# Hybrid decoder step on one Trainium2 core: router logits and expert tokens taken from x before its norm, during the output projection, and the down bias added in the last expert group

## The chip, the cores and the metric

The kernel runs on one core of one Trainium2 chip. The metric is the device time of one execution in microseconds (us). TensorE (PE) multiplies, VectorE (DVE) and ScalarE (ACT) work elementwise and drain PSUM, GpSimd (POOL) builds constants, and SyncE (SP) issues the weight transfers, which 16 DMA engines carry out.

## The reference

One layer for 256 prompt tokens and 8 single-step samples, 264 tokens together, 1024 channels, all float32. What matters here is the stage between the mixing branches and the experts, and the experts:

```python
x = x + jnp.einsum("bld,de->ble", g_a * branch_a + g_b * branch_b, w_out)
hm = _rmsnorm(x, norm_ffn).reshape(b * l, D_MODEL)
# in _moe(hm, ...):
logits = x2d.astype(jnp.float32) @ w_router.astype(jnp.float32) + b_router.astype(jnp.float32)
top_v, top_i = lax.top_k(logits, TOP_K)
top_w = jax.nn.softmax(top_v, axis=-1)
gates = jnp.sum(jax.nn.one_hot(top_i, N_EXPERTS, dtype=jnp.float32) * top_w[..., None], axis=1)
for e in range(N_EXPERTS):
    gu = x2d @ w_gate_up[e] + b_gate_up[e]
    gate = jnp.minimum(gu[:, :D_FF], SWIGLU_LIMIT)
    up = jnp.clip(gu[:, D_FF:], -SWIGLU_LIMIT, SWIGLU_LIMIT)
    hid = (up + 1.0) * (gate * jax.nn.sigmoid(SWIGLU_ALPHA * gate))
    ye = hid @ w_down[e] + b_down[e]
    out = out + gates[:, e:e + 1] * ye.astype(jnp.float32)
```

`_rmsnorm` divides a token by the root of the mean of its squares and multiplies by a gain per channel. 4 of 32 experts are taken per token. After the experts come a gated per-layer embedding and a last norm.

## The kernel before

**Layout.** Activations stand transposed: 128 channels on the partitions, 8 blocks `k` of channels, 264 tokens along the free side (`xT`, `aT`, `zT`). For the router and the gather they are also wanted with tokens on the partitions: three blocks `j` of 88 tokens (`TB`, `NTB`).

**PSUM.** Each of the 8 banks has a written-out order of uses (`plan(name, bank)`); `to_fill` waits until the bank's use before is drained, `fill_done` tells that it is filled, and `to_drain` and `wait_drained` are the other side. On DVE and ACT nearly every instruction is followed by a wait for itself (`tell`, `out_of`).

**Weights.** A ring of 12 slots of 1 MB. SP issues the loads in order. Three slots serve `w_in`, `w_conf_out`, `w_gdn_out` and `w_out`; the other nine are filled with the first chunks of experts 0 and 1 from load 32 of the stream on, and the last three follow as chunks of `w_out` come free (L539 to L541). From then on each load waits for the chunk that held its slot 12 loads ago (`chunk_used`). An expert is 12 chunks: 8 of `w_gate_up`, 4 of `w_down`. The loads of group 1 and later first wait for `order_ready` (L543), since the order of the experts is data.

**Between the branches and the experts.** PE computes `wo`, the output projection, as eight blocks of eight matmuls (L846), one bank each. DVE adds each block to `xT` (L1642), ACT squares it (L1111). Then, each after the one before: PE sums the squares over channels by a matmul with ones (L612), ACT takes the root (L1117), DVE the reciprocal and the eight normed blocks `aT` (L1392, L1394). PE computes the logits as 24 matmuls with 88 x 128 weights (L863) and transposes `aT` into 88-token blocks (L870), which ACT copies to `hm_tok` (L1286). DVE adds the router bias and takes the top four (L1650 to L1662, `sel`), ACT exponentiates (L1290), DVE normalizes to `gates`. PE transposes the gates (L875), counts each token's rank within its expert (L883, L885), and multiplies the 32 x 264 gates with the down biases `b_down`, eight matmuls that DVE adds to `xT` (L891, L1755). DVE builds one-hot rows of the ranks (L1693), and PE gathers the 64 tokens of each of the first two experts (L907). ACT makes a rounded copy of the gate-up bias (L1292), DVE the low part (L1759). DVE then picks the two busiest experts and their places (L1769 to L1790), which gives `order_ready`.

**Experts.** 17 groups: 15 of two experts with 64 token slots each, and groups 6 and 11 with one expert and 128 slots. In a group PE adds the bias (L929), multiplies with the gate-up chunks (L937: x as weights of 64 columns, one expert on either half of the array), gathers for the next group (L907), transposes the hidden rows (L948), adds the outputs of the group before back to their tokens (L990, the scatter, in two parts), and multiplies with the down chunks (L969). DVE clips and multiplies, and adds the scattered rows to `xT` (L1749).

## Time and profile before

| | us |
|---|---|
| median of 3 runs | 1619.56 (1614.94 to 1626.01) |
| the profiled execution | 1626.19 |
| its span, first to last instruction | 1624.5 |
| PE busy | 1480.3 (91%) |
| DVE busy | 505.9 (31%) |
| ACT busy | 251.7 (15%) |
| POOL busy | 49.0 (3%) |
| HBM read | 455.75 MB |

Times of instructions are from the start of the span. Overlapping matmuls are each given their whole pass through the array, so a group's busy time, or the distance between starts, tells more of its price than the mean of one. A float32 matmul shows as two instructions, a float32 transpose as one.

### The profile page before, as it was taken

What the parts mean: (1) busy time and instruction counts of PE and PEld (TensorE: products, weight loads), DVE (VectorE), ACT (ScalarE), POOL (GpSimd) and SP (SyncE); (2) the same over time, 40 slices, a digit from 0 to 9 for tenths busy, and PEclk for the clock granted to TensorE, in tenths of its full rate; (3) what the DMA queues carried; (4) which work ended last, traced back from release to release, by engine and by line L of the source; (5) the groups of instructions that cost most, each with busy time, mean ns of one, the idle gap of its engine ahead of it and who ended that gap; (6) DMA issues with size and microseconds to landing.
All of it is one profiled execution on the core that took longest, in us unless ns stands there. A gap on an engine that the chain in (4) does not pass through costs nothing.

```text
span 1624.5 us, 19637 instructions
## 1 busy us (share of the span) xinstructions
PE 1480.3 (91%) x7317; PEld 863.8 (53%) x7317; DVE 505.9 (31%) x1074; ACT 251.7 (15%) x502; POOL 49.0 (3%) x68
## 2 busy tenths in 40 slices
PE   3899999889999799989989999998999999889777
PEld 3587777677788644433443444444344434424356
DVE  1366677786521321211210221121022102202222
ACT  2341424223220201000100100010010101001022
POOL 2010101111000000000000000000000000000000
PEclk8798999999999779999999999999999999999989
DMA  6132414232259149999999999999998999999920
GB/s 181 52 105 66 121 53 133 68 105 90 79 185 333 49 201 420 421 422 423 421 422 422 421 381 357 421 422 422 422 421 352 386 421 421 422 423 421 407 71 27
DMA packets 120447, 462.62 MB, mean 285 GB/s; under 512 B 9783, under 2 KB 68680, under 8 KB 71128
## 3 DMA queue, kind: packets, MB, share of 16 engines
q1 hardware_dynamic: 100304, 447.97, 68.9%
q10 hardware_dynamic: 20080, 13.82, 3.0%
q8 instruction: 39, 0.64, 0.2%
q14 instruction: 24, 0.20, 0.0%
HBM read 455.75 MB, written 6.68 MB: 285 GB/s over the span
## 4 chain that ended last, share of the span: by engine, by line
PE 71%; DMA 14%; DVE 9%; ACT 2%; issue 2%; ACTq 1%; SPq 0%; POOL 0%; DVEq 0%; POOLq 0%
PE bank L937 19%; PE bank L969 15%; DMA ring<-in_w_gate_up 14%; PE bank L802 9%; PE bank L907 6%; PE bank L846 4%; PE bank L990 4%; PE bank L674 2%; PE bank L1034 2%; DVE lent L1570 1%; PE bank L612 1%; PE bank L929 1%; ACTq L1065 1%; PE bank L680 1%; PE bank L948 1%
## 5 line engine op out<-in xcount | busy, mean ns | idle before, releaser
L937 PE MATMUL bank<-ring,lent 128*64 128x512 f32 x2176 | 482.3, 596 | 50.2 <-DMA ring<-in_w_gate_up 50.1
L937 PEld LDWEIGHTS bank<-ring,lent 128*64 128x64 f32 x2176 | 159.0, 137 | 365.1 <-issue 348.1
L969 PE MATMUL bank<-ring,lent 128*64 128x512 f32 x1088 | 241.0, 595 | 0.2 <-ACT lent L1324 0.2
L802 PE MATMUL bank<-lent,ring 128*128 128x264 f32 x896 | 237.7, 410 | 3.4 <-DVE big L1591 1.6
L802 PEld LDWEIGHTS bank<-lent,ring 128*128 128x128 f32 x896 | 172.2, 203 | 38.8 <-issue 8.0
L1731 DVE TENSOR_SCALAR big<-bank 128x512 f32<-128x512 f32 x34 | 21.9, 686 | 476.9 <-PE bank L937 476.9
L969 PEld LDWEIGHTS bank<-ring,lent 128*64 128x64 f32 x1088 | 75.1, 137 | 143.5 <-issue 135.9
L1318 ACT ACTIVATE big<-big 128x512 f32<-128x512 f32 x34 | 20.9, 630 | 545.1 <-DVE big L1731 545.1
L907 PEld LDWEIGHTS bank<-st,big 88*128 88x128 f32 x816 | 97.3, 200 | 14.5 <-issue 14.5
L907 PE MATMUL bank<-st,big 88*128 88x128 f32 x816 | 100.6, 286 | 0.8 <-DVE xT L1755 0.8
L1749 DVE TENSOR_TENSOR xT<-xT,bank 128x264 f32<-128x264 f32 x136 | 58.3, 429 | 102.5 <-PE bank L990 100.9
L990 PE MATMUL bank<-outputs 128*128 128x264 f32 x272 | 69.5, 401 | 1.2 <-ACT outputs L1310 1.2
L674 PEld LDWEIGHTS bank<-ring 128*128 128x128 f32 x448 | 61.9, 205 | 14.5 <-DVE ring L1482 9.0
L1686 DVE CAST selector<-eye_order 64x64 fp32r (+1 forms) x32 | 4.9, 186 | 206.7 <-PE bank L937 206.7
L674 PE MATMUL bank<-ring 128*128 128x128 f32 x448 | 63.7, 290 | 5.9 <-DVE ring L1482 4.8
L1570 DVE SCALAR_TENSOR_TENSOR lent<-lent,wdw 128x256 f32<-128x256 f32 x120 | 63.2, 527 | 4.3
L1310 ACT COPY outputs<-bank 128x512 f32<-128x512 f32 x34 | 18.2, 588 | 295.1 <-PE bank L969 295.1
L990 PEld LDWEIGHTS bank<-outputs 128*128 128x128 f32 x272 | 50.5, 195 | 22.4 <-issue 13.0
L846 PE MATMUL bank<-lent,ring 128*128 128x264 f32 x192 | 43.2, 387 | 1.1 <-DVE lent L1639 1.1
L846 PEld LDWEIGHTS bank<-lent,ring 128*128 128x128 f32 x192 | 36.3, 190 | 7.7 <-DVE lent L1639 1.5
L1034 PE MATMUL bank<-lent,ring 128*128 128x264 f32 x128 | 32.3, 409 | 4.4 <-DVE lent L1394 4.4
L680 PE MATMUL bank<-ident,ring 128*128 128x128 f32 x128 | 20.6, 290 | 13.6 <-DVE ring L1476 9.3
(304 smaller groups left out, 1104.6 us busy)
## 6 DMA issues: line engine op xcount, KB each, us to landing
ring<-in_w_gate_up SPq DMA_DIRECT2D x256, 1024.0 KB, 17.5
ring<-in_w_down SPq DMA_DIRECT2D x128, 1024.0 KB, 23.4
ring<-in_w_in SPq DMA_DIRECT2D x28, 1024.0 KB, 5.3
st<-in_state_gdn ACTq DMA_DIRECT2D x8, 512.0 KB, 5.6
out<-st ACTq DMA_DIRECT2D x8, 512.0 KB, 3.5
ring<-in_w_gdn_out SPq DMA_DIRECT2D x4, 1024.0 KB, 5.2
ring<-in_w_out SPq DMA_DIRECT2D x4, 1024.0 KB, 10.8
ring<-in_w_ple_gate SPq DMA_DIRECT2D x4, 1024.0 KB, 17.6
```

Of the source, the lines that this page charges most:

```text
L674: last = mm(b[:, i * P:(i + 1) * P], lhs(i), rhs(i), start=True, stop=True)
L680: last = tr(b[:, i * P:(i + 1) * P], src(i), ident[:])
L802: last = mm(b[:, 0:T], w[:, k, o:o + P], aT[:, k, :], start=k == 0, stop=k == KD - 1)
L846: last = mm(b[:, 0:T], w[:, k, o:o + P], rhs(k), start=k == 0, stop=k == n_k - 1)
L907: last = mm(aux[h][:, i * SLOTS:(i + 1) * SLOTS], hm_tok[0:TB, j, k * P:(k + 1) * P], onehot[:, j, :], start=j == 0, stop=j == NTB - 1)
L937: last = mm(bank[t][rows, :], x_slots[:, c, rows], w, start=False, stop=c == KD - 1)
L969: last = mm(bank[4 + t][rows, :], hT[:, m, rows], w, start=m == 0, stop=m == KD - 1)
L990: mm(bank[SCATTER_BANKS[i]][:, 0:T], y[:, i * P:(i + 1) * P], spread, start=True, stop=True).then_inc(sm["sc_filled"], 1)
L1034: last = mm(b[:, 0:T], w[:, k, P * (i % 2):P * (i % 2) + P], aT[:, k, :], start=k == 0, stop=k == KD - 1)
L1570: tell(v.scalar_tensor_tensor(x, up[:, i, tap:tap + TP], w, x, ALU.mult, ALU.add), "conf_done" if t == CK * CB - 1 else None)
L1731: v.tensor_scalar(half(gbuf, h), bank[h][:], LIMIT, None, ALU.min).then_inc(sm["gate_in"], 1)
L1749: v.tensor_tensor(xT[:, i, :], xT[:, i, :], bank[SCATTER_BANKS[i]][:, 0:T], ALU.add).then_inc(sm["sc_added"], 1)
```

## The change

- `wo` uses banks 0 and 1 in turn. After each block PE transposes the block before it. What is transposed is `xg`, which ACT makes of `xT` and the gain `norm_ffn`, without the root (`tokens_of`, 3 transposes a block).
- The logits are made of `xg` with `w_router` as weights of 32 columns; block `k` goes to columns and PSUM rows 32 (k mod 4). DVE copies the four partial rows to `lq`, and three short matmuls with a stacked identity (`eye4`) add and transpose them.
- DVE squares and sums over the blocks during `wo`; the sum over channels is six matmuls that move two columns. ACT takes the root of 88 x 3 values and DVE the reciprocal. The factor enters as the scale of the six `hm_tok` copies and of the logits.
- The rounded bias and its low part are made while `wo` runs; DVE waits for it at block 3.
- The ranks come before the gates, with seven matmuls in place of nine; the offset `FAR` stays in the ranks and in `iota`, which takes away a DVE instruction. The gates are finished, and transposed, behind the first gather in PE's order.
- The matmuls of the down bias move into the last group, one behind each pair of gate-up chunks, and DVE adds them there. `b_down` lies elsewhere and is loaded after the exponentials.

```diff
-        for name in ("bb", "ba", "wo"):
+        for name in ("bb", "ba"):
             for i in range(KD):
                 plan(f"{name}{i}", i)
+        for i in range(KD):
+            plan(f"wo{i}", i % 2)
...
-            dense("wo", "out", 2, KD, lambda k: aT[:, k, :])
-            sum_squares("rms2", 2)
+            def tokens_of(k):
+                pe.wait_ge(s["xg_ready"], k + 1)
+                for j in range(NTB):
+                    name = f"hm{2 * j + k // 4}"
+                    b = to_fill(pe, name) if k % 4 == 0 else bank[uses[name][0]][:]
+                    x = tr(b[0:TB, (k % 4) * P:(k % 4 + 1) * P], xg[:, k, j * TB:(j + 1) * TB], ident[:])
+                    if k % 4 == 3:
+                        fill_done(name, x)
+            def raw_logits(b, k):
+                q = slice(NE * (k % 4), NE * (k % 4 + 1))
+                return mm(b[q, 0:T], wr[:, k, :], xg[:, k, :], start=k < 4, stop=k >= 4)
+            for i in range(KD):
+                w = take_chunk(pe, "out", i // 2)
+                b = to_fill(pe, f"wo{i}")
+                o = P * (i % 2)
+                for k in range(KD):
+                    last = mm(b[:, 0:T], w[:, k, o:o + P], aT[:, k, :], start=k == 0, stop=k == KD - 1)
+                fill_done(f"wo{i}", last)
+                if i:
+                    tokens_of(i - 1)
+            lqb = to_fill(pe, "lq")
+            for k in range(KD - 1):
+                raw_logits(lqb, k)
+            pe.wait_ge(s["xg_ready"], KD)
+            fill_done("lq", raw_logits(lqb, KD - 1))
+            pe.wait_ge(s["squares"], KD + 1)
+            b = to_fill(pe, "ss")
+            for j in range(NTB):
+                cols_j = slice(j * TB, (j + 1) * TB)
+                mm(b[0:TB, 2 * j:2 * j + 2], sq_sum[:, cols_j], ones[:, 0:2], start=True, stop=False)
+                last = mm(b[0:TB, 2 * j:2 * j + 2], sq_last[:, cols_j], ones[:, 0:2], start=False, stop=True)
+            fill_done("ss", last)
+            tokens_of(KD - 1)
+            wait_drained(pe, "lq")
             b = to_fill(pe, "logits")
             for j in range(NTB):
-                for k in range(KD):
-                    if j == 0:
-                        wait_block(2, k)
-                    last = mm(b[0:TB, j * NE:(j + 1) * NE], aT[:, k, j * TB:(j + 1) * TB], wr[:, k, :],
-                              start=k == 0, stop=k == KD - 1)
+                last = mm(b[0:TB, j * NE:(j + 1) * NE], lq[:, j * TB:(j + 1) * TB], eye4[:], start=True, stop=True)
...
+            pe.wait_ge(s["selected"], 1)
             b = to_fill(pe, "rank")
...
-            for i in range(KD):
-                b = to_fill(pe, f"bd{i}")
-                fill_done(f"bd{i}", mm(b[:, 0:T], b_down[:, i * P:(i + 1) * P], gatesT[:], start=True, stop=True))
...
+            def down_bias(i):
+                if i >= 2:
+                    pe.wait_ge(s["bd_added"], i - 1)
+                mm(aux[i % 2][:, 0:T], b_down[:, i * P:(i + 1) * P], gatesT[:],
+                   start=True, stop=True).then_inc(s["bd_filled"], 1)
...
+                    if end:
+                        if c == 0:
+                            pe.wait_ge(s["bd_loaded"], 16 * 3)
+                        down_bias(c)
...
             gather(first, 0)
+            pe.wait_ge(s["gates"], 1)
+            b = to_fill(pe, "gTr")
+            for j in range(NTB):
+                last = tr(b[0:NE, j * TB:(j + 1) * TB], gates[:, j, :], ident[0:TB, 0:TB])
+            fill_done("gTr", last)
             pe.wait_ge(s["bias_ready"], 1)
...
             act.wait_ge(s["mix"], KD)
-            act.dma_start(b_down, a["b_down"][0]).then_inc(s["bd_loaded"], 16)
...
-            squares(zT, lambda k: wait_drained(act, f"wo{k}"))
-            root(rstd[:], "rms2", 1.0 / D)
+            for k in range(KD):
+                wait_drained(act, f"wo{k}")
+                A(xg[:, k, :], xT[:, k, :], ACT.Copy, scale=par[:, 8 + k:9 + k]).then_inc(s["xg_ready"], 1)
+                if k == 1:
+                    act.wait_ge(s["bd_loaded"], 16 * 2)
+                    nc.scalar.copy(bias, b_stage).then_inc(s["b_high"], 1)
+                if k == 2:
+                    tell(A(small8[:, 3:4], small8[:, 0:1], ACT.Sqrt, scale=0.0))
+            out_of(A(root_t, to_drain(act, "ss")[0:TB, 0:2 * NTB].rearrange("t (j two) -> t j two", two=2)[:, :, 0],
+                     ACT.Sqrt, bias=eps[0:TB, 0:1], scale=1.0 / D), "ss")
+            act.wait_ge(s["rstd_ready"], 1)
...
+                if end:
+                    dve.wait_ge(sm["sc_added"], n * KD - KD)
+                    for i in range(KD):
+                        dve.wait_ge(s["bd_filled"], i + 1)
+                        v.tensor_tensor(xT[:, i, :], xT[:, i, :], bank[6 + i % 2][:, 0:T], ALU.add).then_inc(s["bd_added"], 1)
+                    dve.wait_ge(s["bd_added"], KD)
                 dve.wait_ge(sm["chunk_used"], at * RING + (2 * KD if kind == PAIR else KD))
```

## Rows read from the trace of the kernel before

**Rows 1.** The page: 40 slices of 40.6 us, DMA busy in tenths, and GB/s
```profile
DMA  6132414232259149999999999999998999999920
GB/s 181 52 105 66 121 53 133 68 105 90 79 185 333 49 201 420 421 422 423 421 422 422 421 381 357 421 422 422 422 421 352 386 421 421 422 423 421 407 71 27
```
**Rows 2.** The chain that ended last, in the experts: start us, us, what
```profile
698.96 22.41 DMA ring<-in_w_gate_up
...
758.58 22.46 DMA ring<-in_w_gate_up
...
1315.39 27.62 PE bank L937 x128
```
**Rows 3.** Timeline, 480 to 600 us: start, us, engine, line, op, shapes, count, idle before
```profile
504.93 28.75 PE L846 MATMUL bank<-lent,ring 128*128 128x264 f32 x128 [1.06 <-DVE lent L1639]
...
530.22 0.43 DVE L1642 TENSOR_TENSOR xT<-xT,bank 128x264 f32<-128x264 f32 x1 [3.13 <-PE bank L846]
...
533.51 3.72 PE L612 MATMUL bank<-big,ones 128*128 128x264 f32 x16
...
541.67 7.93 PE L863 MATMUL bank<-wr,lent 128*88 128x32 f32 x48 [4.43 <-DVE lent L1394]
...
549.42 4.14 PE L870 MATMUL bank<-ident,lent 128*88 128x128 f32 x24
549.74 0.63 DVE L1650 TENSOR_TENSOR st<-bank,brt 88x32 f32<-88x32 f32 x3 [5.39 <-PE bank L863]
...
552.41 0.25 DVE L1662 TENSOR_TENSOR st<-st 88x96 f32<-88x96 f32 x1
...
557.07 1.90 ACT L1292 CAST moe<-big 64x2048 fp32r<-64x2048 f32 x1
...
558.23 0.62 PE L875 MATMUL bank<-ident,st 88*32 88x88 f32 x3 [4.67 <-DVE st L1667]
...
561.73 7.40 PE L891 MATMUL bank<-outputs,big 32*128 32x264 f32 x16
...
562.66 0.62 DVE L1693 TENSOR_TENSOR st<-st 88x192 f32<-88x192 f32 x2
...
569.70 2.28 DVE L1759 TENSOR_TENSOR moe<-big,moe 32x2048 fp32r<-32x2048 f32 x1
...
569.92 10.36 PE L907 MATMUL bank<-st,big 88*128 88x128 f32 x47 [0.79 <-DVE xT L1755]
...
581.22 2.04 PE L929 MATMUL bank<-moe,selector 64*128 64x512 f32 x4 [0.72 <-issue]
...
588.40 4.24 SPq L504 DMA_DIRECT2D ring<-in_w_gate_up  x4
```
**Rows 4.** Issues of DMA at 505 us: KB each, median us to landing
```profile
big<-in_b_gate_up ACTq DMA_DIRECT2D x2, 256.0 KB, 8.7
```
**Rows 5.** Stretches of 1 us: busy of PE, PEld, DVE, ACT, POOL, granted clock, DMA, GB/s
```profile
541.00:542.00 1.00, 0.33 (x3) 0.25 (x3) 0.97 (x3) 0.00 (x0) 0.00 (x0) 0.97 0.00 0
...
552.00:553.00 1.00, 1.00 (x10) 0.98 (x9) 0.59 (x4) 0.70 (x3) 0.00 (x0) 0.91 0.00 0
...
555.00:556.00 1.00, 0.00 (x0) 0.00 (x0) 0.00 (x0) 1.00 (x1) 0.00 (x0) 0.80 0.00 0
...
586.00:587.00 1.00, 1.00 (x8) 0.26 (x6) 0.00 (x0) 0.00 (x0) 0.00 (x0) 0.84 0.00 0
```
**Rows 6.** Timeline, group 15, at the full clock
```profile
1462.03 5.62 PE L907 MATMUL bank<-st,big 88*128 88x128 f32 x48
...
1475.79 0.39 PE L984 MATMUL bank<-ident,st 88*128 88x88 f32 x3
```
**Rows 7.** Chain, 250 to 260 us: a product of 128 columns that moves 512
```profile
257.61 1.91 PE bank L791 x4
```
**Rows 8.** Timeline, last group
```profile
1521.88 1.29 DVE L1731 TENSOR_SCALAR big<-bank 128x512 f32<-128x512 f32 x2 [44.58 <-PE bank L937]
...
1537.62 10.52 PE L969 MATMUL bank<-ring,lent 128*64 128x512 f32 x48
```

More of the change, by code:

```diff
@@ L52 @@
 BIG = 3.0e38
+FAR = 10000.0
 CHUNK_COLS = 2048
@@ L884, in _ @@
+            mm(b[0:TB, NE:3 * NE], before[:], sel[:, 1:3, :].rearrange("t j e -> t (j e)"), start=True, stop=False)
+            mm(b[0:TB, NE:3 * NE], ones[0:TB, 0:TB], sel[:, 0, :].unsqueeze(1).broadcast_to([TB, 2, NE]), start=False, stop=False)
+            mm(b[0:TB, 2 * NE:3 * NE], ones[0:TB, 0:TB], sel[:, 1, :], start=False, stop=True)
             for i in range(NTB):
@@ L917, in wait_loaded, with group @@
                 pe.wait_ge(sems[slot], at * 16 + 16 * (i // RING + 1 + prefilled[slot]))
-            def group(sm, sems, prefilled, n, at, kind, first, last_one):
+            def down_bias(i):
[3 more added lines that the diff above has]
+                   start=True, stop=True).then_inc(s["bd_filled"], 1)
+            def group(sm, sems, prefilled, n, at, kind, first, last_one, end=False):
                 experts = 2 if kind == PAIR else 1
@@ L1007, in _ @@
             n = GROUPS - 1
-            group(first, loaded, slot_fills, n, round_of(n, shift_of(n)), PAIR, False, True)
+            group(first, loaded, slot_fills, n, round_of(n, shift_of(n)), PAIR, False, True, True)
             last_scatter(first, GROUPS)
@@ L1709, in pair_halves, with group @@
                 return [(pos, low), (pos + 1, low)]
-            def group(sm, n, at, kind, halves, after, first, last_one):
+            def group(sm, n, at, kind, halves, after, first, last_one, end=False):
                 own = [0]
@@ L1752, in _ @@
             make_selector(first, eye2, 0, 1)
-            for i in range(KD):
-                b = to_drain(dve, f"bd{i}")
-                out_of(v.tensor_tensor(xT[:, i, :], xT[:, i, :], b[:, 0:T], ALU.add), f"bd{i}")
-            dve.wait_ge(s["b_high"], 1)
-            low_rows = slice(NE, 2 * NE)
-            tell(v.tensor_tensor(bias[low_rows], b_stage[low_rows], bias[low_rows].bitcast(FP32), ALU.subtract), "bias_ready")
+            b = to_drain(dve, "rank")
+            out_of(v.tensor_copy(count_row, b[0:TB, NTB * NE:(NTB + 1) * NE]), "rank")
+            dve.wait_ge(s["wexp"], NTB)
+            tell(v.tensor_tensor(gates[:], gates[:], sel[:], ALU.mult))
+            tell(v.tensor_reduce(wsum[:], gates[:], AX.X, ALU.add))
+            tell(v.reciprocal(wsum[:], wsum[:]))
+            tell(v.tensor_tensor(gates[:], gates[:], wsum[:].unsqueeze(2).broadcast_to([TB, NTB, NE]), ALU.mult), "gates")
             wait_drained(dve, "gTr")
@@ L1770, in _ @@
                 for other in WIDE_AT[:i]:
-                    tell(v.memset(key[:, other:other + 1], -far))
+                    tell(v.memset(key[:, other:other + 1], -FAR))
                 tell(v.tensor_reduce(key_max[:], key[:, FREE:], AX.X, ALU.max))
```

115 lines of the change are left out of this document (58 added, 57 removed).

## The prediction

> **What bounds the kernel.** I read the page by slices first, then the chain that ended last, then the timeline of the one place where both DMA and PE stand low. From 609 us to about 1540 us the DMA engines move 421 to 423 GB/s, with a dip at each of the two wide groups [rows 1]. The chain says the same from the other side: a pair group ends in a wait for a gate-up chunk, and these waits lie 758.58 - 698.96 = 59.62 us apart, which is 24 chunks of 1 MB at 2.48 us, 422 GB/s [rows 2]. PE at full clock would need less: 27.62 us for the gate-up part of a group, about 53 us with the rest [rows 2]. So the expert phase is a fixed amount of transfer behind one starting point. Where PE leads it (around the wide groups), PE too started from that point.
>
> The starting point is the first load behind the prefilled ring, issued at 588.40 us, when PE has used the first pair of chunks [rows 3]. Slices 14 and 15 show what lies before it: 49 and 201 GB/s [rows 1]. The projection ends at 504.93 + 28.75 = 533.68 us. From there to 588.40 are 54.7 us in which nearly nothing is loaded, and whatever comes off them comes off the end. That the stream is the bound afterwards makes this certain, since no engine has to be faster later.
>
> **The change, part by part.** I keep the old times and call T the end of the projection, 533.7.
>
> *In the projection.* Six groups of three transposes now stand inside it. At full clock three of nearly this form took 0.39 [rows 6], so 6 x 0.39 = 2.3; at low clock 24 took 4.14 [rows 3], so 3.1. Each needs the block before added (0.43) and scaled (about the same, an ACT pass over 264 columns), against a block of 28.75 / 8 = 3.6 [rows 3]: ready. Two banks in place of eight also suffice for the same reason. DVE gets three passes a block, 1.3 of some 4.0. At block 3 it waits for ACT's rounded bias: loads issued at 505.3 land 8.7 later [rows 4], at 514, ACT's 1.9 ends near 517, block 3 is there at 520. DVE's low part of 2.3 [rows 3] then fits before block 4 plus one. If it didn't, two banks would stall PE by at most those 2.3. Root table and one-time loads hide here too. New end of the projection: T' = 536.0.
>
> *Behind it on PE.* Three transposes, 0.4. Then eight raw logits, 16 instructions moving 264 columns. One after another they cost what the projection's do, 28.75 / 128 = 0.225 each, 3.6. On column tiles they may overlap: 512 columns cost 1.91 / 4 = 0.48 in the form with 128 columns [rows 7] and 27.62 / 128 = 0.22 on two halves [rows 2], a factor of two shown. Four tiles give 0.9 at best. I take 1.5, nearer to the overlapped end, because that row has the same mechanism. The last block is scaled at T' + 1.1, before its turn. At T' + 1.9 follow the sums of squares, 12 instructions with 88-column weights: L863's took 7.93 / 48 = 0.165, some of it waits [rows 3], so 1.3 to 2.0, taken as 1.5. With the last three transposes T' + 3.8. Beside them run the copy of the partial logits (0.43), the root (0.3) and the reciprocal (0.2). The three short products, six instructions of the same kind, 1.0, bring it to T' + 4.9 with a signal of 0.1.
>
> *The choice.* DVE needed 549.74 to 552.66 [rows 3], 2.9; two small instructions move out of the way, 2.6 left: T' + 7.5. The ranks no longer wait for the gates. Before, 21 instructions for gates and ranks ran from 558.23 to 561.73 [rows 3], 0.17 each; 14 now, two of them twice as wide, 2.6: T' + 10.2. Rank and one-hot on DVE, 0.25 + 0.62 + 0.1 [rows 3]: T' + 11.2 = 547.2. The `hm_tok` copies, six of 0.6 from T' + 4.2, are done by T' + 8. The exponentials (table 1.3, then 1.0) and gates end beside the gather, so they cost nothing; without that cover they would cost the 4.7 of idle PE that stood before L875 [rows 3].
>
> *Gone from here:* the sum of squares (3.7), root, reciprocal and first normed block (4.4 idle), the logits (7.9), the transposes (4.1), 4.7 of wait for gates, and the down bias (7.4) [rows 3]. The gather starts at 547.2 in place of 569.92: **22.7 earlier**.
>
> *Added behind the gather.* ACT's order is gates first, gathered tokens second. The first half of the tokens was copied during the gather; now both wait behind the transposes of the gates: 0.62 [rows 3], gates copy 0.37, and one more copy of 0.58. So **1.5 later**. DVE selects the wide experts after the gates' copy, near 559 to 567; its order is needed only for chunk 24, twelve chunks behind the first load, near 590, so it stays hidden. Leaves 21.2 for the first load.
>
> *Last group.* PE waits for gate-up chunks there, so seven of the eight products (0.45 each, 264 columns twice) lie in waits. The last stands behind the last chunk, and DVE adds before it clips: 0.45 + 0.1 + 0.43. DVE started its clip at 1521.88, released by PE's last gate-up product [rows 8], and from here PE and not DMA runs the chain: 10.52 us of down products follow [rows 8] with their chunks landed. So **1.0 later**.
>
> Sum: 22.7 - 1.5 - 1.0 = 20.2. The profiled execution took 1626.19, so 1606.0; it stood 6.6 above the median of the runs, and against that median, 1619.56, I forecast **1599.4**.
>
> **The clock.** The granted clock fell at 541.9 us, 4.7 us after PE had ended its sum of squares at 537.2, rose at 552.2, fell at 555.6 in the wait for the gates, and rose only at 586.3, three us into the first gate-up products [rows 5] (each worked out from the mean of the microsecond in which it changed). The whole gather ran at 1.2 GHz: 10.36 us against 5.62 at 2.4 GHz [rows 3, 6]. The sum keeps it so, since the new order too has a DVE wait of 2.6 and one of 1.0 just before it. If the clock held, the gather would give 4.7, bias 0.8, first chunks 1.5, and small ones 0.3: 7.3 more.
>
> **The rivals.**
>
> *A, the forecast*, 1594 to 1604: chance 0.62.
>
> *B, the clock holds through the gather*: 20.2 + 7.3 = 27.5, time 1592. For it: the waits are shorter than the 4.4 and 4.7 before. Against it: even 20 us of nearly unbroken PE work, 561.7 to 581, did not bring the clock back. 0.12.
>
> *C, the tiles don't overlap and the projection stretches*: raw logits 3.6 in place of 1.5, DVE's bias work 2.3, transposes 0.8: 5.2 less, time 1604.6. For it: no row shows 32-column tiles. 0.13.
>
> The Trainium skill (TensorEngine Tiling (Array Packing), Tiling Modes, Key Properties) says that changing the tiling mode drains the engine, and that tiles within a mode run in parallel. It speaks against putting one short tiled piece between full-width ones; with its best case the raw logits cost 0.9 and with no overlap 3.6, the two ends used above from rows.
>
> *D, part of the gain is not carried through*, by the last group (a clip later by several us because DVE's adds queue up) or by a transfer: time 1606 to 1616. Against it: DMA is busy in all slices after the start. 0.09.
>
> *E, the other side: the clock stays low far into group 0.* PE then needs 2 x 53 = 106 us a pair group, DMA 59.62, so each us at low clock starves the stream of 0.44. From 20.2 / 0.44 = 46 us of it on the kernel is slower; one low group costs 47, time 1646. Against it: the clock rose three us into the same instructions [rows 5]. 0.04.
>
> The Trainium skill (TensorE: Matmul & The Clock Gate, Seeing it yourself) reports a clock seen stuck low for over 50 us; no row here shows that.
>
> **How the numbers follow.** The likeliest case gives 1599.4. At best, B with the tiles at 0.9 and the sums at 1.3, 28.3 come off, 1591; at worst, C with the sums at 2.0, 14.5, 1605. The three runs before spread 11 us around their median, so I add half of that above and a little below: 1588 to 1611. One per cent, 16.2 us, is what a measurement can tell: faster by more means under 1603.4: all of B, nearly all of A, two fifths of C, 0.12 + 0.60 + 0.05 = 0.77; D and the rest of A and C within, 0.18; E and a tail of D slower, 0.05.
>
> **What would show it.** In the changed profile: projection 31 us in place of 28.75; under 13 us from its end to the gather; raw logits near 1.5; gather 10.4 (A) or 5.6 (B); the first load behind the ring near 567; 59.6 between pair groups unchanged; clip in the last group 1 us behind the last chunk. The forecast is wrong if a wait stands at block 3 of the projection, if the first load is not earlier by as much as the end is, or if the clock's low stretch changes its length.

## The result: 1599.03 us, and the profile after

| | before | after |
|---|---|---|
| median of 4 runs, us | 1618.16 (1614.94 to 1626.01) | 1599.03 (1596.92 to 1602.02) |
| the profiled execution, us | 1626.19 | 1598.15 |
| its span | 1624.5 | 1596.3 |
| ratio of the runs | | 0.9876, 95% interval 0.9836 to 0.9916 |

The changed kernel is faster by 1.2% (0.8 to 1.6%); small, but the interval excludes no gain. Of the two profiled executions one span is 28.2 us shorter than the other, more than the 19.1 us between the medians; the sections below take that apart.

The page of the changed kernel, 40 slices of 39.9 us, answers to [rows 1]:

```profile
DMA  6132324232249289999999989999998999999920
GB/s 184 49 110 67 111 66 123 67 106 83 67 159 370 87 349 421 421 422 422 422 422 422 421 348 390 421 421 422 422 422 346 389 422 422 422 422 421 412 93 28
```

The stream is the same, 421 and 422 GB/s with two dips. Slice 15, 201 GB/s before, has become 349. The stage in front of it, timeline of the changed kernel (start us, us, engine, line, operation, shapes, count), answers to [rows 3]:

```profile
503.52 7.39 PE L882 MATMUL bank<-lent,ring 128*128 128x264 f32 x32 [1.06 <-DVE lent L1689]
...
520.19 2.28 DVE L1707 TENSOR_TENSOR moe<-big,moe 32x2048 fp32r<-32x2048 f32 x1
...
522.68 0.43 DVE L1696 TENSOR_TENSOR xT<-xT,bank 128x264 f32<-128x264 f32 x1 [0.21 <-PE bank L882]
...
530.52 3.73 PE L882 MATMUL bank<-lent,ring 128*128 128x264 f32 x16
...
534.50 1.52 PE L875 MATMUL bank<-outputs,wr 128*32 128x264 f32 x16
...
536.91 0.51 PE L868 MATMUL bank<-ident,outputs 128*88 128x128 f32 x3
...
537.26 0.58 PE L902 MATMUL bank<-eye,outputs 128*88 128x32 f32 x6
...
540.47 0.25 DVE L1726 TENSOR_TENSOR st<-st 88x96 f32<-88x96 f32 x1
...
541.91 1.47 PE L913 MATMUL bank<-st,ones 88*128 88x32 f32 x6
...
544.55 10.58 PE L930 MATMUL bank<-st,big 88*128 88x128 f32 x48 [1.17 <-DVE st L1749]
...
557.33 2.04 PE L959 MATMUL bank<-moe,selector 64*128 64x512 f32 x4 [1.76 <-ACT lent L1354]
...
564.00 4.25 SPq L511 DMA_DIRECT2D ring<-in_w_gate_up  x4
```

The projection (L882) runs from 503.52 to 530.52 + 3.73 = 534.25. DVE's low part of the bias (L1707) ends at 522.47, just before block 4 is there at 522.68, and PE does not wait. Raw logits (L875), last transposes (L868), joined logits (L902), choice (L1726) and ranks (L913) follow, and the gather (L930) starts 10.3 us behind the projection; before it was 36.2. The gather takes 10.58 us, as long as before, where all its 48 instructions take 10.58 too (the row in [rows 3] holds 47 of them and 10.36). The first load behind the ring is issued at 564.00.

The granted clock, in stretches of 1 us of the changed kernel, answers to [rows 5]:

```profile
540.00:541.00 1.00, 0.18 (x2) 0.21 (x3) 0.82 (x5) 0.97 (x2) 0.00 (x0) 0.96 0.00 0
...
561.00:562.00 1.00, 1.00 (x6) 0.38 (x4) 0.93 (x3) 0.00 (x0) 0.00 (x0) 0.80 0.00 0
```

It fell to 1.2 GHz at 540.9 and came back at 561.4: one low stretch of 20.5 us in place of two, 541.9 to 552.2 and 555.6 to 586.3, 41.0 us together.

The tail of the changed kernel, the chain from the last gate-up products on (start us, us, what), answers to [rows 8]:

```profile
1493.75 3.65 PE bank L967 x16
1497.41 0.65 PE bank L946 x2
...
1498.08 0.44 DVE xT L1789
...
1498.55 1.29 DVE big L1793 x2
...
1504.99 3.67 PE bank L1024 x12
...
1532.20 3.81 PE bank L619 x16
...
1540.44 5.49 PE bank L1075 x16
```

The same chain in the kernel before:

```profile
1518.18 3.67 PE bank L937 x16
...
1521.88 1.29 DVE big L1731 x2
...
1528.33 4.45 PE bank L990 x12
...
1556.68 6.70 PE bank L612 x16
...
1567.81 6.25 PE bank L1034 x16
```

The down bias (L946) and its add (L1789) are on the chain: the clip (L1793) comes 4.80 us behind the start of the last gate-up products, before 3.70. But three PE steps behind it are shorter, the scatter (3.67 for 4.45), the sum of squares (3.81 for 6.70) and the first gate block (5.49 for 6.25), none of which the change touches.

### The profile page after: what moved, and what is told of

It reads as the page before. It is cut to its first block, busy times and chain, and to the rows that moved or that the text cites. A ratio compares the mean times of both kernels' runs of the same rounds, so it can differ in the third digit from the quotient of the medians.

```text
span 1596.3 us, 19577 instructions
## 1 busy us (share of the span) xinstructions
PE 1462.8 (92%) x7283; PEld 847.4 (53%) x7283; DVE 507.9 (32%) x1080; ACT 253.2 (16%) x503; POOL 49.7 (3%) x71
## 4 chain that ended last, share of the span: by engine, by line
PE 72%; DMA 14%; DVE 8%; ACT 2%; issue 2%; ACTq 1%; SPq 0%; POOL 0%; DVEq 0%; POOLq 0%
PE bank L967 19%; PE bank L1003 15%; DMA ring<-in_w_gate_up 14%; PE bank L809 9%; PE bank L930 6%; PE bank L1024 4%; PE bank L853 3%; PE bank L681 2%; PE bank L1075 2%; PE bank L882 2%; DVE lent L1620 1%; PE bank L959 1%; ACTq L1106 1%; PE bank L687 1%; PE bank L982 1%
## 5 line engine op out<-in xcount | busy, mean ns | idle before, releaser
L809 PE MATMUL bank<-lent,ring 128*128 128x264 f32 x896 | 237.2, 410 | 3.3 <-DVE big L1641 1.6
L809 PEld LDWEIGHTS bank<-lent,ring 128*128 128x128 f32 x896 | 171.8, 202 | 38.4 <-issue 8.1
L1793 DVE TENSOR_SCALAR big<-bank 128x512 f32<-128x512 f32 x34 | 21.9, 686 | 430.6 <-PE bank L967 430.5
L930 PEld LDWEIGHTS bank<-st,big 88*128 88x128 f32 x816 | 97.3, 200 | 14.3 <-issue 14.3
L930 PE MATMUL bank<-st,big 88*128 88x128 f32 x816 | 100.6, 286 | 1.2 <-DVE st L1749 1.2
L1075 PE MATMUL bank<-lent,ring 128*128 128x264 f32 x128 | 31.5, 402 | 4.4 <-DVE lent L1444 4.4
L687 PE MATMUL bank<-ident,ring 128*128 128x128 f32 x128 | 20.2, 287 | 13.0 <-DVE ring L1526 9.3
L1224 ACT COPY ring<-bank 128x512 f32<-128x512 f32 x20 | 11.7, 586 | 126.1 <-PE bank L687 126.1
L882 PE MATMUL bank<-lent,ring 128*128 128x264 f32 x128 | 29.7, 387 | 1.1 <-DVE lent L1689 1.1
```

The source lines that it names most:

```text
L687: last = tr(b[:, i * P:(i + 1) * P], src(i), ident[:])
L809: last = mm(b[:, 0:T], w[:, k, o:o + P], aT[:, k, :], start=k == 0, stop=k == KD - 1)
L882: last = mm(b[:, 0:T], w[:, k, o:o + P], aT[:, k, :], start=k == 0, stop=k == KD - 1)
L930: last = mm(aux[h][:, i * SLOTS:(i + 1) * SLOTS], hm_tok[0:TB, j, k * P:(k + 1) * P], onehot[:, j, :], start=j == 0, stop=j == NTB - 1)
L1075: last = mm(b[:, 0:T], w[:, k, P * (i % 2):P * (i % 2) + P], aT[:, k, :], start=k == 0, stop=k == KD - 1)
```

## The experiments

The ledger below is read from every profile in the same way: start of the output projection, start of the first gather, first load behind the ring, start of the last gate-up products, end of the span. Each row is one execution, in us.

| kernel | projection starts at | to gather | to first load | first load to last gate-up | from there to the end | span |
|---|---|---|---|---|---|---|
| before | 504.93 | 64.99 | 83.47 | 929.78 | 106.32 | 1624.5 |
| e1, before again | 503.83 | 65.00 | 83.49 | 930.01 | 106.07 | 1623.4 |
| after | 503.52 | 41.03 | 60.48 | 929.75 | 102.55 | 1596.3 |
| e2, one column tile | 503.54 | 43.50 | 63.38 | 930.17 | 102.91 | 1600.0 |
| e3, bias ahead of group 0 | 499.31 | 41.10 | 68.79 | 929.79 | 103.81 | 1601.7 |
| e4, wide fillers | 498.88 | 39.90 | 52.26 | 932.02 | 107.84 | 1591.0 |
| e5, gates first | 504.16 | 46.13 | 65.87 | 929.99 | 107.18 | 1607.2 |
| e6, two orders mended | 499.58 | 41.11 | 59.70 | 930.03 | 105.89 | 1595.2 |
| e7, e4 and e6 and tail | 503.43 | 39.91 | 51.84 | 930.68 | 101.65 | 1587.6 |
| e8, before with fillers | 495.31 | 61.74 | 80.24 | 929.82 | 109.53 | 1614.9 |
| e9, narrow fillers | 503.94 | 40.48 | 61.11 | 929.90 | 105.45 | 1600.4 |
| e10, before, bias last | 503.10 | 58.74 | 77.47 | 930.39 | 102.94 | 1613.9 |

The second and third columns count from the projection's start. The fourth hardly moves: 929.75 to 930.7 in eleven of twelve, 932.0 in one. The first and the fifth move by up to 9.6 and 7.9 us, also between kernels whose code there is the same. The second and third repeat within 0.02 us in the two profiles of the kernel before.

**e1: the kernel before, profiled again.** No edit.

> The kernel before, profiled a second time, unchanged. In the first pair of profiles the changed kernel gained 23.0 us between the start of the output projection and the first load behind the ring, nothing from there to the last gate-up chunk (929.78 and 929.75 us), and 3.8 us in the tail behind that chunk, where I had forecast a loss of 1.0. Theory 1 (the tail's gain is the phase of PE's clock in that one execution): this second profile has a tail, from the last gate-up product to the end of the span, that differs from the first one's 106.3 us by more than a microsecond, and shows the sum of squares behind the experts at 3.8 in place of 6.7 us or the like. Theory 2 (the change causes the gain): the tail is 106.3 within 0.5 again. Under both the stretch from projection start to first load is 83.5 within 1, and the stream 929.8 within 1.

Measured: the stage 83.49 and the stream 930.01, as both theories had it. The tail is 106.07, 0.25 from the first profile, and its sum of squares 6.73. So theory 1's test failed: two executions of one kernel agreed. Theory 2 could claim it until e5, whose tail code is that of the changed kernel and whose chain reads

```profile
1539.15 6.84 PE bank L619 x16
...
1550.42 6.32 PE bank L1075 x16
```

with a tail of 107.18, against 3.81 and 5.49 in the changed kernel and the same 3.81 and 5.49 in e2, whose tail code is the same again. The short tail is no property of the change. Added up from stretches of 1 us, the clock stood low for some 27 us of the tail in e5 and in the kernel before, and for 17 to 18 in the changed kernel and in e2.

**e2: the raw logits on one column tile.**

```diff
-                q = slice(NE * (k % 4), NE * (k % 4 + 1))
-                return mm(b[q, 0:T], wr[:, k, :], xg[:, k, :], start=k < 4, stop=k >= 4)
+                return mm(b[0:NE, 0:T], wr[:, k, :], xg[:, k, :], start=k == 0, stop=k == KD - 1)
```

(the copy to `lq` and the joining products take 32 rows)

> The changed kernel with all eight raw logit products on column tile 0, accumulated in 32 rows of PSUM, in place of four tiles. Theory 1 (tiles overlap): the group took 1.52 us on four tiles and takes 3.6 us on one (16 instructions at the projection's 0.225), so the sums of squares, the logits, the gather and the first load all come 2.1 us later. Theory 2 (the last block's arrival sets it, or the moving side runs at the same rate anyway): it stays within 0.5 us of 1.52 and nothing moves.

Timeline of e2:

```profile
534.52 3.75 PE L874 MATMUL bank<-outputs,wr 128*32 128x264 f32 x16
```

3.75 for 1.52 us, the gather 2.47 later, the first load 2.9, the span 3.7 longer than that of the changed kernel (its tail is 0.4 longer). The tiles overlap. Of the 1.52 us in the changed kernel, 0.3 are a wait for ACT's scaling of the last block (L1325 ends at 535.34, the last product's weights follow); on one tile that block is there in time. The gather moves by slightly more than the products' 2.23.

**e3: the down bias back ahead of group 0**, behind the first gather:

```diff
             pe.wait_ge(s["bias_ready"], 1)
+            pe.wait_ge(s["bd_loaded"], 16 * 3)
+            wait_drained(pe, "gTr")
+            for i in range(KD):
+                if i >= 4:
+                    pe.wait_ge(s["bd_added"], i - 3)
+                mm(bank[2 + i % 4][:, 0:T], b_down[:, i * P:(i + 1) * P], gatesT[:],
+                   start=True, stop=True).then_inc(s["bd_filled"], 1)
+            pe.wait_ge(s["bd_added"], KD)
```

(DVE adds them there; they are gone from the last group)

> The changed kernel with the down bias taken out of the last group and put behind the first gather, ahead of group 0 (eight products into banks 2 to 5, added by DVE). Theory 1 (what stands before the first load costs the end one for one, and the bias in the last group costs 1.1): the eight products take 7.4 us at the low clock, some 1.7 of which hide the copies of the gathered tokens, so the first load comes 5.7 us later, the clip in the last group 1.1 earlier, and the execution is 4.6 us longer. Theory 2 (the products in the last group keep the clock up and so gain in the tail): the tail behind the last gate-up product goes from 102.5 back to 106.3 in addition, some 8.4 us longer in all.

```profile
551.99 7.37 PE L1043 MATMUL bank<-outputs 32*128 32x264 f32 x16 [0.55 <-ACT outputs L1347]
...
559.88 2.07 PE L959 MATMUL bank<-moe,selector 64*128 64x512 f32 x4 [0.52 <-DVE xT L1825]
```

The products take 7.37 us (timeline of e3). The first load comes 8.3 later, 2.6 more than expected: group 0 starts 6.8 later, since less of the products was hidden than the 1.7 I had set, and from there to the load it took 8.22 in place of 6.67, because the clock was still low at 567. The clip is 3.70 behind the last gate-up products again, 1.1 earlier. The tail is 103.8, not 106.3 or more. The median of four is 1604.92, ratio to before 0.9905 (0.9868 to 0.9942). Theory 1 holds, with its size too small; theory 2 falls.

**e4: wide fillers in PE's waits.**

```diff
+            b = to_fill(pe, "rank")
+            for i in range(6):
+                mm(b[:, 0:T], ident[:], aT[:, i, :], start=True, stop=True)
             pe.wait_ge(s["selected"], 1)
...
             fill_done("rank", last)
+            b = to_fill(pe, "gTr")
+            for i in range(2):
+                mm(b[:, 0:T], ident[:], aT[:, i, :], start=True, stop=True)
...
             fill_done("gTr", last)
+            for i in range(3):
+                mm(bank[3][:, 0:T], ident[:], aT[:, i, :], start=True, stop=True)
```

(`b` is the bank that the next real product overwrites)

> The changed kernel with products whose results are thrown away in PE's three waits: six between logits and ranks, two between ranks and gather, three behind the transposes of the gates (128 x 128 identity by 264 tokens, 0.45 us each at full clock). Theory 1 (the idle time at 537.8 to 540.8 is what drops the clock at about 540.9): the clock stays up, the ranks take 1.8 in place of 2.6, the gather 5.6 in place of 10.6, the bias products 1.2 in place of 2.0 and the first pair of chunks 3.7 in place of 4.7; the first load comes 7 us earlier and the end with it. Theory 2 (small products such as ranks and gather drop the clock whatever stands between them): the gather is still 10.4 to 10.6 and, as fillers at the low clock are twice as long, the first load is 0 to 2 us later.

Timeline of e4:

```profile
536.77 0.83 PE L915 MATMUL bank<-st,ones 88*128 88x32 f32 x6
...
538.78 5.60 PE L935 MATMUL bank<-st,big 88*128 88x128 f32 x48 [0.20 <-DVE st L1756]
...
546.37 1.17 PE L964 MATMUL bank<-moe,selector 64*128 64x512 f32 x4 [0.39 <-ACT lent L1361]
```

A stretch of 1 us just before the gather (columns as in [rows 5]):

```profile
538.00:539.00 1.00, 0.80 (x5) 0.42 (x4) 0.95 (x5) 0.96 (x3) 0.00 (x0) 1.00 0.00 0
```

The clock stays up, although PE still stands for a fifth of this microsecond. The gather takes 5.60 and the first load comes 8.2 us earlier. This is the price of the low clock in the changed kernel, up to the first load. At the last gate-up products 5.95 of the 8.22 are left (932.02 for 929.75 in the stream). Of four executions the median is 1593.44, ratio 0.9818 (0.9774 to 0.9861); the profiled one lost 5.3 of its gain in the tail, where its sum of squares took 6.86.

**e5: the gates ahead of the ranks.**

```diff
             fill_done("logits", last)
+            pe.wait_ge(s["gates"], 1)
+            b = to_fill(pe, "gTr")
+            for j in range(NTB):
+                last = tr(b[0:NE, j * TB:(j + 1) * TB], gates[:, j, :], ident[0:TB, 0:TB])
+            fill_done("gTr", last)
...
             gather(first, 0)
-            pe.wait_ge(s["gates"], 1)
...
```

(DVE finishes the gates before it takes the ranks)

> The changed kernel with the gates finished and transposed ahead of the ranks, as before, in place of behind the first gather. Theory 1 (hiding the exponentials beside the ranks and the gather is a term of its own): PE waits until the gates at 545.3 in that trace, then transposes of the gates 0.6, ranks 2.6, one-hot 1.0: the gather starts 5.2 us later; behind it the gates' transposes and copy are gone, 1.0 to 1.5 earlier; the first load comes 3.7 to 4.2 later. Theory 2 (ACT's copies of the tokens set the gather's start anyway, so the order of gates costs nothing): the first load moves by less than 1.

```profile
546.13 0.62 PE L908 MATMUL bank<-ident,st 88*32 88x88 f32 x3 [7.66 <-DVE st L1732]
```

PE stands for 7.66 us (timeline of e5) and the gather starts 5.1 later. Behind it 1.3 come back up to group 0, and 1.6 go again because the first gate-up products run longer at the low clock: the first load is 5.4 later. Theory 1 holds; the expectation left the clock out.

**e6: the two losses mended.** ACT copies the gathered tokens before the gates, and `down_bias(c)` stands ahead of the wait for chunk pair `c`:

```diff
-            out_of(nc.scalar.copy(gatesT, to_drain(act, "gTr")[0:NE, 0:T]), "gTr")
             gathered(first, 0)
+            out_of(nc.scalar.copy(gatesT, to_drain(act, "gTr")[0:NE, 0:T]), "gTr")
...
                 for c in range(KD):
+                    if end:
+                        if c == 0:
+                            pe.wait_ge(s["bd_loaded"], 16 * 3)
+                        down_bias(c)
                     for x in range(experts):
```

> The changed kernel with the two terms that my sum had as losses put right: ACT copies the gathered tokens before the gates, and in the last group each product of the down bias stands ahead of its chunk's wait in place of behind its products. Theory 1 (both losses are order alone): from the gather's start to the first load 18.3 in place of 19.45 us, and from the last gate-up product's start to the clip 3.7 in place of 4.8. Theory 2 (the extra products and PE's transposes of the gates cost what they cost wherever they stand): both stay.

From the gather to the first load 18.59 (59.70 - 41.11) in place of 19.45, and the clip 3.77 behind the start of the last gate-up products in place of 4.80. Theory 1 holds, in one execution: both losses were a matter of order, to within 0.3 and 0.1 us of its figures.

**e7: e4 and e6, and nine fillers in each of three waits of the tail.**

```diff
+                elif end:
+                    pe.wait_ge(s["bd_added"], KD)
+                    fill_time(aux[0], 9)
...
             sum_squares("rms3", 2)
+            fill_time(to_fill(pe, "pg0"), 9)
...
             sum_squares("rms4", 3)
+            fill_time(to_fill(pe, "y00"), 9)
```

(`fill_time(b, n)`: n products of the 128 x 128 identity by 264 columns of a constant into bank `b`)

> e6 and e4 together, and thrown-away products in three waits of the tail (nine each: behind the last gate-up product, between the sum of squares and the gates of the embedding, and before the last transposes). Theory 1 (in the tail as ahead of the experts the waits of 3 to 5 us drop the clock, at a point that differs from execution to execution): first load 8.2 + 1.1 earlier than in the changed kernel, counted from the projection's start; last scatter 2.7, sum of squares 3.8 and first gate block 3.6 us in every execution, tail 98.5 to 99.5 in place of 102.5; the median near 1585. Theory 2 (the fillers delay as much as the clock gives in the tail): tail 102 or more, median 1590 or more.

The chain of e7:

```profile
1495.79 2.67 PE bank L1038 x12
...
1522.45 6.71 PE bank L625 x16
...
1533.59 3.80 PE bank L1092 x16
```

The scatter (2.67) and the first gate block (3.80) run at 2.4 GHz behind their fillers. The sum of squares, whose own wait of 3.6 us I had left open, takes 6.71, with the clock low from 1521.5 to 1528.3, so the tail is 101.65 and not 99.5. The fillers stand in three waits, and the clock was up behind each set; behind the third the last transposes end 4.8 us after they start, in the changed kernel 6.3. It fell in the wait of 3.6 us that has none. Theory 1 comes out for two of its three figures and for the median, and not for the sum of squares and the tail; theory 2 asked for a median of 1590 or more. The median of six is 1585.98 (1584.07 to 1589.38), ratio to before 0.9778 (0.9756 to 0.98). Against the same measure of the changed kernel, 0.9876 in other runs, that is another 1% off. It is the lowest ratio of the kernels here, but its interval touches that of e4 (0.9774 to 0.9861), so that the two orders of e6 and the fillers of the tail gain anything beside e4 is not shown by the totals.

**e8: the kernel before with wide fillers alone**, nine ahead of its logits and twelve ahead of the gates' transposes.

> The kernel before, with thrown-away products alone: nine behind its sum of squares and twelve ahead of the gates' transposes. This asks how much of the old 54.7 us was the clock and how much the order of work. Theory 1 (the old stage was slow largely by the clock): logits, transposes, ranks and down bias and gather run at 2.4 GHz, 2.9 + 1.5 + 1.1 + 3.5 + 4.8 us and 2.3 for the first products of group 0, some 16 us earlier first load, median near 1606. Theory 2 (weight loads and DVE set these steps, so the clock matters for the gather and group 0 alone): 7 us, median near 1615.

Timeline of e8:

```profile
531.96 7.06 PE L870 MATMUL bank<-wr,lent 128*88 128x32 f32 x48 [0.34 <-DVE lent L1402]
538.84 4.70 PE L877 MATMUL bank<-ident,lent 128*88 128x128 f32 x24
...
550.61 5.63 PE L899 MATMUL bank<-outputs,big 32*128 32x264 f32 x16
...
557.05 10.58 PE L915 MATMUL bank<-st,big 88*128 88x128 f32 x48 [0.82 <-DVE xT L1763]
```

Four stretches of 1 us of e8 (columns as in [rows 5]):

```profile
534.00:535.00 1.00, 0.88 (x7) 0.65 (x7) 0.74 (x2) 0.00 (x0) 0.00 (x0) 1.00 0.06 16
535.00:536.00 1.00, 1.00 (x15) 1.00 (x15) 0.00 (x0) 0.00 (x0) 0.00 (x0) 0.96 0.00 0
...
542.00:543.00 1.00, 1.00 (x8) 0.94 (x7) 0.09 (x1) 0.73 (x2) 0.00 (x0) 0.62 0.00 0
...
553.00:554.00 1.00, 1.00 (x4) 0.77 (x3) 0.93 (x3) 0.00 (x0) 0.00 (x0) 0.50 0.00 0
```

Only 3.2 us off the stage, ratio 0.9989 (0.997 to 1.0007), no measurable gain in the total. The long wait before L870 is gone (0.34 us is left of 4.43), and within the logits PE stood only for 0.1 to 0.2 us in each of the three microseconds in which DVE was still making the normed blocks. Yet the clock fell at 535.9, four us into the logits, with PE busy throughout that microsecond; it rose at 542.8, within the transposes of `aT`, and fell again at 553, in the middle of the down bias. Neither theory foresaw this: the long wait for DVE is not needed for a fall.

**e9: narrow fillers**, the test of that sentence. As e4, with

```diff
+            for i in range(17):
+                mm(b[0:TB, 0:NE], ident[:, 0:TB], ones[:, 0:NE], start=True, stop=True)
```

and 6 and 9 of them in the two later places.

> e4 with small products in place of wide ones in the same three waits, for about the same busy time: 17, 6 and 9 products of 88 columns that move 32 (the shape of the logits in the kernel before) in place of 6, 2 and 3 of 128 columns that move 264. Theory 1 (PE's idle time drops the clock): it stays up, the gather takes 5.6 us and the first load comes 52 us after the projection's start, as in e4. Theory 2 (a stretch filled only with products of this shape drops the clock as idle time does; in e8 it fell four us into the logits although PE had not stood still before them): the clock falls at about the same place as in the changed kernel, the gather takes 10.6 us, and the first load is at 60 to 62 us.

Timeline of e9:

```profile
538.11 2.83 PE L908 MATMUL bank<-ones,ident 128*88 128x32 f32 x34
...
544.42 10.59 PE L935 MATMUL bank<-st,big 88*128 88x128 f32 x48
```

Two stretches of 1 us of e9 (columns as in [rows 5]):

```profile
541.00:542.00 1.00, 0.79 (x10) 0.79 (x10) 0.32 (x2) 0.97 (x2) 0.00 (x0) 1.00 0.00 0
542.00:543.00 1.00, 1.00 (x10) 1.00 (x9) 0.03 (x1) 0.98 (x2) 0.00 (x0) 0.69 0.00 0
```

The clock fell at 542.4 (0.69 = 0.38 x 1 + 0.62 x 0.5) in a microsecond in which PE was busy throughout, 1.5 us later than in the changed kernel. Counted from the end of the projection it fell 7.7 us on, in the changed kernel, e2, e3, e5 and e6, which have no fillers, 6.3 to 6.9, and in e4 and e7, with the wide ones, not at all. The gather took 10.59 us, as without any filler, and the first load came 61.11 behind the projection's start: e4 52.26, the changed kernel 60.48. In this trace PE being busy was not enough: it was busy in every microsecond from 543 to 562, all of them at 1.2 GHz. With the wide products of e4 the clock stayed up, with the narrow ones it fell. Theory 2 holds, theory 1 falls, in one execution of e9. The two sets of fillers differ in their data too (activations in e4, ones in e9); the wide fillers of e7's tail move a constant, and the clock was up behind all three sets, which speaks for the shape, but shape and data were not separated in these three waits.

**e10: the kernel before with the down bias in the last group**, one part of the change alone.

```diff
-            pe.wait_ge(s["bd_loaded"], 16 * 3)
-            wait_drained(pe, "gTr")
-            for i in range(KD):
-                b = to_fill(pe, f"bd{i}")
-                fill_done(f"bd{i}", mm(b[:, 0:T], b_down[:, i * P:(i + 1) * P], gatesT[:], start=True, stop=True))
...
+                    if end:
+                        if c == 0:
+                            pe.wait_ge(s["bd_loaded"], 16 * 3)
+                        down_bias(c)
```

(`down_bias` and DVE's adds as in the changed kernel)

> One part of the change alone: the kernel before with the down bias in the last group. Theory 1 (this part is worth its own time ahead of the gather and nothing else): the gather starts 6.6 us earlier (64.99 us after the projection's start becomes 58.4: 7.4 of products and 0.8 of the last drain, less what DVE's one-hot needed behind the ranks), the first load too (83.5 becomes 76.9), and the clip in the last group is 1.1 later. Theory 2 (DVE's low part of the gate-up bias, 2.3 us, which ran beside the gather, moves onto the path, or the gather now runs at the full clock since nothing cold stands before it): 74.5 or less with a gather of 5.6, or 79 or more.

Timeline of e10:

```profile
558.74 1.47 PE L883 MATMUL bank<-st,ones 88*128 88x32 f32 x6
...
561.84 10.58 PE L900 MATMUL bank<-st,big 88*128 88x128 f32 x48 [1.63 <-DVE st L1697]
562.05 2.28 DVE L1765 TENSOR_TENSOR moe<-big,moe 32x2048 fp32r<-32x2048 f32 x1
```

The gather starts 58.74 behind the projection's start, 6.3 earlier than before; the first load 77.47, 6.0 earlier. Theory 1 holds for both, within 0.6 us: DVE's low part of the bias (L1765) still runs beside the gather, as in the kernel before, and the gather still takes 10.58. The clip stands 4.80 behind the last gate-up products, 1.1 later. One execution took 1615.67, beside 1616.56 for the kernel before, so the total alone says nothing of a gain; the ledger does. Of the 23.0 us that the first load moved, 6.0 are the down bias, measured alone; the other 17.0 are the rest of the change, of which e2 and e5 take back two parts (2.9 and 5.4 us).

## Why the forecast came out

By its own steps, each in the two profiled executions and counted from the start of the projection:

| step | forecast, us | measured, us |
|---|---|---|
| projection longer | 2.3 | 2.0 (28.75 to 30.73) |
| raw logits | 1.5 | 1.52 |
| sums of squares | 1.5 | 1.1 |
| joining products | 1.0 | 0.58 |
| DVE's choice | 2.6 | 2.77 |
| ranks | 2.6 | 2.56 |
| rank and one-hot | 1.0 | 1.06 |
| end of projection to gather | 11.2 | 10.3 |
| gather earlier | 22.7 | 23.96 (64.99 - 41.03) |
| lost behind the gather | 1.5 | 0.97 (19.45 - 18.48) |
| first load earlier | 21.2 | 22.99 (83.47 - 60.48) |
| lost in the last group | 1.0 | 1.10 (4.80 - 3.70) |
| sum | 20.2 | 21.9 |

**The starting point.** This step carried the forecast, and it held: from the first load to the last gate-up products it is 929.78 us before and 929.75 after. Whatever moved the load moved the last gate-up products within 1 us, in every kernel of the ledger but e4, where 2.3 of 8.2 us were given back on the way (932.02); where, was not followed.

**The projection.** The worry at block 3 was unfounded by a narrow margin: L1707 ended at 522.47, and DVE took block 4 at 522.68, as soon as PE had it. DVE had 0.2 us to spare there, and PE no wait.

**The tiles.** The guess of 1.5 lay between 0.9 and 3.6, and e2 measured what one tile costs, 3.75. So four tiles ran 2.5 times as fast (3.75 / 1.52). Rival C asked for no overlap; e2 is that part of it, and it stood 2.9 us later at the first load, where 2.1 had been worked out. The Trainium skill (TensorEngine Tiling (Array Packing), Overview, Theoretical Speedup) gives up to 4x for a dimension of at most 32; the 2.5 measured here lies below it. Of the 1.52 us, 0.3 are the wait for the last scaled block, so without it, by subtraction, the products would take 1.2, a factor of 3.1. The drain that it names for a change of mode (same page, Tiling Modes, Key Properties) did not show as a gap of any size: the raw logits started 0.25 us after the projection's end, with three transposes between.

**The end of the projection to the gather** came out 0.9 shorter than forecast. Two terms were too large, the sums of squares (1.1 for 1.5) and the joining products (0.58 for 1.0), and both by one price: 12 and 6 short instructions at L863's 7.93 / 48 = 0.165 us [rows 3]. I had put a part of that down to waits, which is right: until 544.4 DVE was still making the normed blocks, and PE began 6 or 7 instructions a microsecond; e8, at full clock, shows the same 6 or 7 until DVE is done. The other part I had left out: L863 ran at 1.2 GHz nearly from its start, since the clock fell at 541.9. Behind DVE's last block it did 9 a microsecond, and the same line in e8 did 15 at full clock (535 to 536). The new products wait for nothing of this kind and run ahead of the fall: 1.1 / 12 = 0.09 and 0.58 / 6 = 0.10. The rank products, priced by rows at the low clock and run at it, came out as forecast; in e4, at the high one, the last six of them took 0.83 in place of 1.47.

**Behind the gather** I took 1.5 for the gates in front of the copy; e6, which turns the two around, gives 0.86 (19.45 - 18.59) for the same order. The net loss of 0.97 is close to that.

**The last group**, 1.0 forecast and 1.10 measured, is confirmed from three sides: e3 (without it) 3.70, e6 (products put ahead of the wait) 3.77, e10 (with it, in the kernel before) 4.80.

**The clock.** Case A kept the gather at 1.2 GHz, and it took 10.58 us. Case B, the clock held, did not come by itself; e4 brought it about, and its price was 8.2 us, where 7.3 had been worked out. But the reason I gave was half of it. I had the waits for DVE down as the cause. e4 filled them with wide products and the clock stayed up; e9 filled them with narrow ones, and e8 filled the long wait in the kernel before, and in both it fell while PE was busy. So neither the waits alone nor PE's busy time tells when it falls, and what PE runs in them matters. The columns moved do not sort the cases either: in e8 the clock fell a second time within the down bias, products of 32 rows that move 264 columns, and in e8 and in the kernel before it rose within the transposes of `aT`, 88 columns of weights that move 128 (at 542.8 and 552.2). What it is about the products that matters, the runs do not show. The 20 us of nearly unbroken work before the change, 561.7 to 581, that did not bring the clock back are of the same kind as the 19 in e9 (543 to 562). D and E did not come: no part of the gain was lost to the stream, and the clock rose at 561.4, four us into group 0.

**The signs I had named.** No wait stood at block 3 of the projection. The two other signs that were to show the forecast wrong did appear, as they are worded: the first load came 24.4 us earlier (588.40 to 564.00) and the end of the span 28.2, and the clock's low time went from 41.0 to 20.5 us. The first of them is the tail, taken apart below. The second was badly chosen: the stretch grew shorter with the work that ran in it, while what the sum rested on, a gather and first products of group 0 at 1.2 GHz, came out.

**What the sum left out.** The forecast for the profiled pair was a fall of 20.2 us; it was 28.0 (1626.19 - 1598.15), 28.2 between the spans. The ledger gives the pieces of the 28.2: 21.9 of the change, 3.77 + 1.10 = 4.87 in the tail, and 1.41 by which the projection started earlier. The last two are no part of the change, as far as e5 and the starts show. The starts lie between 495.31 and 504.93, the tails between 101.65 and 109.53, and in the tail the same code, L619 in the changed kernel and in e5, ran 16 products in 3.81 and in 6.84 us. The granted clock from 1541 to 1544 was 0.50 in e5, and around 1533 to 1536 it was 1.00 in the changed kernel. The Trainium skill (TensorE: Matmul & The Clock Gate, What's actually happening) says that the monitor behind the clock runs independently of the kernel, so that the point at which it turns differs from run to run; the traces agree that it differs, with tails of 102.6 (changed kernel), 102.9 (e2) and 107.2 (e5) around code that is the same. That such a monitor is the reason, no run here shows.

**So the median's nearness is partly luck.** 1599.4 was forecast and 1599.03 measured, but the median of before had itself moved by 1.4 between the two sets of runs, 1619.56 to 1618.16, and the fall between medians, 19.1, is smaller than the 21.9 of the ledger. Both carry the scatter of starts and tails; the interval of the ratio, 0.8 to 1.6% of 1618, is 13.6 to 26.5 us and holds either. What stands on firmer ground is the stage: 23 us earlier at the first load, 1.1 given back at the end.

**What stays open.** Why the start of the projection differs by up to 9.6 us was not tested; the kernel before and e8 have the same code up to there and start it at 504.93 and 495.31. The granted clock goes with it: added up from stretches of 1 us, it is low for 44 to 48 us ahead of the projection in the four executions that start it before 500, and for 58 to 75 in the eight that start it after 503. Why the clock turned where it did in the tail of one execution and not of another wasn't tested beyond e7, in whose profile the clock was up behind each of the three sets of fillers in the tail and fell in the wait of 3.6 us without. And from the narrow products that failed and the wide ones that worked no border between them can be read.

## What to carry to other kernels

Before a phase bound by transfer, find the one instruction that starts it; what was taken from the chain ahead of it came off the last gate-up products within a microsecond in all kernels but e4, which gave 2.3 of 8.2 us back, and a per-token norm that commutes with the linear steps behind it is a good thing to take off that chain. Put extra small products ahead of a wait that PE has anyway and not behind it (e6 against the changed kernel), and where short waits stand before long products, look at the granted clock, since a few wide products in the waits gave 8.2 us at the first load (e4), more than the two changes of order in e6 (0.9 and 1.0). Compare two executions by a ledger of stages and not by their spans: here untouched code moved the span by more than some of the edits did.

## What the runs showed of the hardware

- The clock fell while PE was busy with narrow products. In e9 it fell at 542.4 with PE busy for the whole microsecond, within the last rank products, which move 32 columns; in e8 at 535.9, four us into 7.06 us of logits, 88-column weights that move 32 columns. With wide ones, 264 columns against 128-column weights, it stayed up in e4 and e7, and the 48 instructions of the gather, begun at full clock, then took 5.60 us and not 10.58 (e4).
- In e9 PE was busy in every microsecond from 543 to 562, and all of them were at 1.2 GHz.
- The same gather, begun at low clock, ran its 10.6 us without bringing it back; the clock rose only in the gate-up products behind it, at 561.4.
- Eight products with 32-column weights (16 instructions that move 264 columns) took 1.52 us on four column tiles, 0.3 of them a wait for the last block, and 3.75 on one.
